# Joining the chunk products of a recurrent scan in pairs of 128 columns, and masking them in another order

## The reference

```python
def rwkv7_step(S, inp):
    r, w, k, v, kk, kka = inp
    sa = jnp.einsum('dbhij,dbhj->dbhi', S, -kk)
    S = S * w[..., None, :] + sa[..., :, None] * kka[..., None, :] + v[..., :, None] * k[..., None, :]
    y = jnp.einsum('dbhij,dbhj->dbhi', S, r)
    return S, y
...
    S0 = jnp.zeros((N_DIR, B, RWKV_HEADS, HEAD_DIM, HEAD_DIM), jnp.float32)
    _, ys = lax.scan(rwkv7_step, S0, xs)
```

## Time and profile before

| | |
|---|---|
| median of 3 runs | 4080.89 us (4072.22 to 4085.7) |
| the profiled execution, first to last instruction | 4081.7 us |
| TensorE busy | 3554.1 us (87%) |
| VectorE busy | 2039.0 us (50%) |
| the scan within it | from about 2995 to 3266 us |

### The profile page before, as it was taken

One profiled execution on the slowest core, in us unless ns is written; L12 is line 12 of the kernel. 1 busy time (PEld: TensorE's weight loads), 2 busy tenths in 40 slices (PEclk: granted clock), 3 DMA queues, 4 the chain that ended last, 5 costly groups with the idle time before them and its releaser, 6 DMA issues. The chain is left out here.

```text
span 4081.7 us, 57350 instructions
## 1 busy us (share of the span) xinstructions
PE 3554.1 (87%) x23427; PEld 2932.0 (72%) x23427; DVE 2039.0 (50%) x2873; ACT 1248.3 (31%) x1650; POOL 0.2 (0%) x4
## 2 busy tenths in 40 slices
PE   7889999997999998799988799968258768979998
PEld 5667888775888776678866688858157746768886
DVE  3475745436665545553443543443655547235334
ACT  2363423324433323332233332222311033214222
POOL 0000000000000000000000000000000000000000
PEclk9999999997999999899989899979579978989998
DMA  3101222220222221122222122212000010112221
GB/s 129 71 0 62 93 94 102 93 93 11 83 100 96 93 84 63 42 73 102 93 83 82 42 93 94 102 58 81 0 8 4 4 42 1 62 62 93 96 100 62
DMA packets 43842, 280.12 MB, mean 69 GB/s; under 512 B 5967, under 2 KB 7119, under 8 KB 11156
## 3 DMA queue, kind: packets, MB, share of 16 engines
q1 hardware_dynamic: 36576, 266.35, 18.4%
q10 hardware_dynamic: 7092, 11.21, 0.8%
HBM read 275.44 MB, written 2.11 MB: 68 GB/s over the span
## 5 line engine op out<-in xcount | busy, mean ns | idle before, releaser
L164 DVE TENSOR_TENSOR WL<-W,WH 128x2048 fp32r<-128x2048 f32 x254 | 582.1, 2292 | 883.2 <-ACT WH L154 877.6
L231 PE MATMUL PS<-XH,WH 128*128 128x512 f32 x2288 | 894.8, 391 | 3.9 <-issue 2.2
L233 PE MATMUL PS<-XH,WL 128*128 128x512 f32 x2288 | 890.3, 389 | 0.0
L232 PE MATMUL PS<-XL,WH 128*128 128x512 f32 x2288 | 890.2, 389 | 0.0
L154 ACT ACTIVATE WH<-W 128x2048 fp32r<-128x2048 f32 x254 | 485.6, 1912 | 1212.1 <-PE PS L321 679.2
L231 PEld LDWEIGHTS PS<-XH,WH 128*128 128x128 f32 x2288 | 429.5, 188 | 99.4 <-issue 10.9
L232 PEld LDWEIGHTS PS<-XL,WH 128*128 128x128 f32 x2288 | 429.5, 188 | 91.1 <-issue 2.2
L233 PEld LDWEIGHTS PS<-XH,WL 128*128 128x128 f32 x2288 | 429.5, 188 | 89.1
L319 PE MATMUL PS<-HH,WH 128*128 128x512 f32 (+1 forms) x1024 | 401.8, 392 | 10.5 <-DVEq L95 9.3
L320 PE MATMUL PS<-HL,WH 128*128 128x512 f32 (+1 forms) x1024 | 400.2, 391 | 0.0
L321 PE MATMUL PS<-HH,WL 128*128 128x512 f32 (+1 forms) x1024 | 400.0, 391 | 0.0
(11 more groups left out here) (444 smaller groups left out, 4395.2 us busy)
## 6 DMA issues: line engine op xcount, KB each, us to landing
W<-in_weights SPq DMA_DIRECT2D x254, 1024.0 KB, 4.8
X<-in_x ACTq DMA_DIRECT2D x1, 2048.0 KB
out<-X ACTq DMA_DIRECT2D x1, 2048.0 KB, 7.1
bias<-bias_spread ACTq DMA_DIRECT2D x4, 256.0 KB
wide_consts<-in_consts ACTq DMA_DIRECT2D x1, 643.0 KB
w_gd<-in_w_gd ACTq DMA_DIRECT2D x1, 640.0 KB
rope<-in_c_rope ACTq DMA_DIRECT2D x1, 528.0 KB
ws<-in_ws ACTq DMA_DIRECT2D x1, 512.0 KB
```

The costliest lines, as they stand in the source:

```text
L164: P.e.tensor_tensor(K.WL[:, s, :], K.W[:, s, :], K.WH[:, s, :].bitcast(F32), ALU.subtract).then_inc(P.sem("weights_split"), P.adds("weight ...
L231: P.e.matmul(out, wh[:, k, c], xh[:, k, r], start=(k == 0), stop=False)
L232: P.e.matmul(out, wh[:, k, c], xl[:, k, r], start=False, stop=False)
L233: last = P.e.matmul(out, wl[:, k, c], xh[:, k, r], start=False, stop=(k == KT - 1))
```

## The change

The products N move to banks 0 and 1, alone. What else is multiplied by b (ab and rb) is now one product of 64 stationary and 2 x 64 streamed columns, issued at the start of the step; and what is multiplied by k (ak and rk) is another, issued after `late_sums`. The 80 operand products of a full step become 48, of which 32 have 128 columns. On VectorE rb is masked right after `state`, without a wait of its own; rk and ak are masked together, after the second `below` is taken. The semaphore `grams_masked` is given after rb, and again after ak.

```diff
+        def grams(left, c):
+
+            for d, F, t, q, cols in each(c):
+                if c < 0:
+                    out, right = K.PS[t, 6 + d, 64 * q:64 * q + 64], src(c, d, "a", F, q)
+                else:
+                    out = K.PS[t, 6 + d, :].rearrange("p (h q n) -> p h q n", h=2, q=4)[:, :, q, :]
+                    right = K.ar[d][F, 0:2, q, self.tokens(c, d)]
+                last = mm(out, src(c, d, left, F, q), right, start=True, stop=True)
+            last.then_inc(P.sem("grams_done"), P.adds("grams_done"))
+
+        def first_grams(c):
+
+            for d, F, t, q, cols in each(c):
+                mm(K.PS[t, d, cols], src(c, d, "a", F, q), src(c, d, "b", F, q), start=True, stop=True)
+            grams("b", c)
...
             if n is not None:
-                fill(("N", "ab"), n, ("rows_ready",) if full else ())
+                if full:
+                    P.e.wait_ge(P.sem("rows_ready"), P.due("rows_ready"))
+                first_grams(n)
...
             if c is not None:
                 late_sums(c)
-            fill(("rb", "ak") if full else ("ak",), n, ("grams_masked",))
+            P.e.wait_ge(P.sem("grams_masked"), P.due("grams_masked"))
+            grams("k", n)
             P.e.wait_ge(P.sem("inverse_ready"), P.due("inverse_ready"))
             below(n)
-            if full:
-                fill(("rk",), n, ("grams_masked",))
             doubled(n)
...
             if c is not None:
                 state(c)
+            if full:
+                masked(K.c_rb, self.two(K, 6, 1, m), K.c_incl[:, 0:m, :], m).then_inc(P.sem("grams_masked"), P.adds("grams_masked"))
+            else:
+                P.e.sem_inc(P.sem("grams_masked"), P.adds("grams_masked"))
+            below(m, 1)
             P.e.wait_ge(P.sem("grams_done"), P.due("grams_done"))
             if full:
-                masked(K.c_rb, self.two(K, 6, 0, m), K.c_incl[:, 0:m, :], m)
-            masked(K.c_ak, self.two(K, 6, 1 if full else 0, m), K.c_strict[:, 1:1 + m, :], m).then_inc(P.sem("grams_masked"), P.adds("grams_masked"))
-            below(m, 1)
-            if full:
-                P.e.wait_ge(P.sem("grams_done"), P.due("grams_done"))
-                masked(K.c_rk, self.two(K, 6, 0, m), K.c_incl[:, 0:m, :], m).then_inc(P.sem("grams_masked"), P.adds("grams_masked"))
+                masked(K.c_rk, self.two(K, 6, 1, m), K.c_incl[:, 0:m, :], m)
+            masked(K.c_ak, self.two(K, 6, 0, m), K.c_strict[:, 1:1 + m, :], m).then_inc(P.sem("grams_masked"), P.adds("grams_masked"))
             doubled(m)
```

More of the change, by code:

```diff
@@ L1801 @@
     HALVES = [slice(0, 64), slice(64, 128)]
-    FILLS = (("N", "ab"), ("rb", "ak"), ("rk",), ("b_rows", "k_rows"), ("v_rows",))
-    META_FILLS = (("N", "ab"), ("ak",), ("b_rows", "k_rows"), ("v_rows",))
     def dirs(self, c):
@@ L1870, in each, with fill_rows @@
             return [(d, F, t, q, slice(64 * q, 64 * q + 64)) for q in range(4) for d, F, t in self.quads(c)]
-        def fill(kinds, c, freed):
-            for name in freed:
-                P.e.wait_ge(P.sem(name), P.due(name))
+        def fill_rows(kinds, c, freed):
+            P.e.wait_ge(P.sem(freed), P.due(freed))
             for half, kind in enumerate(kinds):
@@ L1878, in fill @@
                     out = K.PS[t, 6 + d, 256 * half + 64 * q:256 * half + 64 * q + 64]
[L1879 to L1885, removed]
+                    last = mm(out, src(c, d, kind, F, q), K.ident[F, F], start=True, stop=True)
+            last.then_inc(P.sem("rows_done"), P.adds("rows_done"))
+        def grams(left, c):
[11 more added lines that the diff above has]
+            grams("b", c)
         def right_side(c):
@@ L1966, in pe @@
                 late_sums(c)
-            fill(("rb", "ak") if full else ("ak",), n, ("grams_masked",))
+            P.e.wait_ge(P.sem("grams_masked"), P.due("grams_masked"))
+            grams("k", n)
             P.e.wait_ge(P.sem("inverse_ready"), P.due("inverse_ready"))
             below(n)
-            if full:
-                fill(("rk",), n, ("grams_masked",))
             doubled(n)
-            fill(("b_rows", "k_rows"), n, ("grams_masked",))
+            fill_rows("bk", n, "grams_masked")
             P.e.wait_ge(P.sem("inverse_ready"), P.due("inverse_ready"))
@@ L1976, in pe @@
             doubled(n, not full)
-            fill(("v_rows",), n, ("rows_ready",))
+            fill_rows("v", n, "rows_ready")
             P.e.wait_ge(P.sem("inverse_ready"), P.due("inverse_ready"))
@@ L1996, in begin @@
             P.e.wait_ge(P.sem("grams_done"), P.due("grams_done"))
[L1997 to L2000, removed]
+            masked(K.c_p[:, 1], self.two(K, 0, 0, n), K.c_first[:, 0:n, :], n)
+            masked(K.c_p[:, 0], self.two(K, 6, 0, n), K.c_first[:, 1:1 + n, :], n)
+            masked(K.c_n, self.two(K, 0, 0, n), K.c_strict[:, 0:n, :], n).then_inc(P.sem("dve_order"), P.adds("dve_order"))
+            P.e.wait_ge(P.sem("dve_order"), P.due("dve_order", 0))
             eye = K.c_eye[:, :].rearrange("p (a n) -> p a n", a=1).broadcast_to([128, 4 * n, 64])
```

## The result

The changed kernel took 4097.3 us (median of 5 runs, 4096.32 to 4099.56). The kernel before took 4082.69 us in the same job (5 runs, 4072.22 to 4086.71). The ratio is 1.0039 with a 95% interval of 1.0029 to 1.005: slower by 0.4%, some 15 us, where 20 were forecast. A second job with the same two kernels gave 1.0055 (the third experiment). The profiled execution took 4094.4 us at a mean granted clock of 0.931.

The account below looks back on a forecast made before the run. It took round trips between TensorE and VectorE to bound the scan. Start +3.3, middle +13.4, meta tokens +0.7, issue waits -2.5 and clock +5 gave +20 us on 4080.9, so 4101 us, range 4087 to 4113.

Parts of the forecast that it names:

- Bound: In the scan: neither engine is full; round trips between TensorE and VectorE lie on a step's path of 28.8 us.
- The price of a joined round: TensorE's 32 joined products: streamed columns set the time, 0.90 us a round against 0.98 for two 64-column rounds.
- The first rival: Joined rounds: second 64 columns are free, a round takes 0.49 us; +8 us, 4089, no change; chance 0.13.
- Start of a step: TensorE's products ahead of the first masks take 1.39 us, not 0.98: +0.4 us a step, +3.3 us in all.
- Middle: From c_rb to the second level's sum: `below` waits behind the k round, +1.67 us a step, +13.4 us in all.
- The second rival: Middle of a step: TensorE comes late to the k round anyway, so not slower; -4 us, 4077; chance 0.06.
- Meta chunk: The 16 meta tokens: their ak round now waits for the sum, +0.7 us once.
- Issue waits: TensorE's waits in the scan that the profile names "issue": fewer instructions lessen them, -2.5 us, bounds 0 and -8.3.
- The clock: TensorE's falls to 1.2 GHz in the scan: three more at 1.7 us each, +5 us.
- the third rival: TensorE's clock falls in every step: eight more falls, 13.6 us; +28 us in all, 4109; chance 0.16.

Follow-up runs that it names:

- the third experiment: The changed kernel run again unchanged, beside the kernel before: 4101.78 us, ratio 1.0055.
- Experiment 1: The changed kernel with the second `below` issued ahead of the wait for c_rb and the k round: 4076.52 us, ratio to the kernel before 0.9988.
- experiment 4: The changed kernel with `state` cut in three, its pieces and other work spread over the step's five levels, `below` ahead of each: 4051.27 us, ratio to before 0.9927.
- 5: The kernel of experiment 4 with its joined products split into two of 64 columns: 4065.35 us, ratio to the kernel before 0.9971.
- 8: The kernel of experiment 4 with only the k round split into products of 64 columns: 4058.95 us, ratio to the kernel before 0.9943.
- 9: The kernel of experiment 4 with 16 more unread products of 64 columns in each full step's closing pause: 4062.11 us, ratio to the kernel before 0.9948.
- experiment 6: The kernel of experiment 4 with rb taken out of the step's start and made late in the step: 4056.48 us, ratio to the kernel before 0.9944.
- 2: The changed kernel, order kept, with joined products split again into two of 64 columns: 4105.11 us, ratio to the kernel before 1.0058.
- 10: The kernel of experiment 4 run again unchanged: 4052.74 us, ratio to the kernel before 0.9928.

## Why the prediction held

**Bound.** It held that both engines' round trips, not either engine's busy time, set the scan. Experiment 1 changes no instruction, only a place in the queue, and gets 25 us; experiment 4 gets 50, by order and by cutting `state` in three. In the layout of 4 a second limit shows, the supply of instructions (5, 8 and 9), which the forecast had only as its issue waits.

**The price of a joined round**, forecast 0.90 us from two rows with more columns: 0.87 and 0.92. The first rival (0.49, the second 64 columns free) is refuted.

**Start of a step**, +0.41 us forecast: 1.69 - 1.28 = 0.41 of idle time ahead of the masks. What the forecast missed is the next link: c_pf to the first c_y took 6.97 us on average before and 6.90 after. Before, two falls of the clock and small waits stood there, so the 0.41 shows in full only against the steps without them (experiment 6). The term can't be read apart from those of the issue waits and the clock.

**Middle**, +1.67 us forecast: 4.77 - 3.13 = +1.64, in six of eight steps; the other two (6.19 and 6.27) hold the clock's two falls. Summed over the steps, c_rb to the sum took 28.7 us before and 41.1 after, +12.4 for a forecast of +13.4; the 28.7 contains four steps of 3.62 to 4.82 us, above the 3.13 of an undisturbed one. Experiment 1 shows the cause: with `below` ahead, the term is gone. The second rival, that TensorE comes late to the k round anyway, is refuted by the 2.40 us for which it stands still there. That rival had named its own condition, `below` ahead of the k round, and with it the kernel came to 4076.5 us, where the rival had put 4077. The match is partly luck: the sum then comes 3.13 us after c_rb and not 2.55, since c_rk waits 0.63 for the k round and c_ak stands ahead of the sum too; fewer issue waits (5.2 us in that scan against 11.2) make up for it.

**Meta chunk**, +0.7 forecast: 18.53 - 16.53 = +2.0. The order costs 0.85: from the start of the sum ahead of the k round to the next c_y it takes 2.56 us (3009.43 to 3011.99), where it took 1.71 (3004.41 to 3006.12). The rest is the clock, which the forecast had left out here. The chunk begins at the low level in both kernels, and it comes back to the full one some 13 us behind c_s's memset before the change and some 16 us behind it now.

**Issue waits**, -2.5 forecast, within bounds of 0 and -8.3: 4.6 - 11.2 = -6.6. The forecast had counted 8.3 of the 11.2, on the two lines hit most. Of what the edit itself sets, this is the term that was most mis-sized. Both of its reasons count: in 2, with the new pauses and the old number of records, the waits are 7.4 us; with 512 records fewer they are 4.6 and 3.8.

**The clock**, three more falls and +5 us forecast: the first profile has 2 falls where before had 6, the second has 8. One costs 1.2 us, not 1.7. A stretch in which TensorE is busy for 0.27 of 3.30 us stands right ahead of the fall at 3217. A pause (2.40 us in the step shown, where the forecast had some 3) is now in each step, yet not each is followed by a fall; the third rival's eight more falls are not borne out. The Trainium skill, TensorE: Matmul & The Clock Gate, HAM oscillation, gives the pauses as the reason; the trace agrees as to where the falls are, not as to how often they come. The term's sign stays open: between two executions of one kernel it moved by 7 us, more than the 5 that the forecast had for it.

The sum for the scan: 3.3 + 13.1 + 2.0 - 6.6 = +11.8, and +7.0 with 1.2 for each of the four falls fewer; measured +9.2 in the first profile. In the second, with 3.8 us of issue waits and two falls more, it is 3.3 + 13.1 + 2.0 - 7.4 + 2.4 = +13.4, and measured 277.9 - 261.7 = +16.2. Two to three us of each stay without an account. The medians of the two jobs give +14.6 and +20.3, that is 4097 and 4102, and 4101 lies between them.

The order and the cost in the middle were right, and so was the price of a joined round. That the total of the first job came within 4 us is in part luck: the issue waits came 4 us and the clock 10 us below what was forecast, while 3.5 us of the profiled difference lie outside the scan, and the kernel before came out at 4082.69 in five runs, 1.8 above the base of the forecast.

## What to carry to other kernels

Joining small products saved instructions here, and hardly any array time: it was worth some 14 us, by the medians, where TensorE used its instructions as fast as they came, and some 3 where it waited for another engine. Whoever reorders masks or signals should list what stands behind each wait in the in-order queue; here one item in front of the critical product cost 1.64 us in each of 8 steps, and swapping the two won it back. A step bound by round trips is shortened by laying independent work into each round trip, one piece for each, and not by making pieces shorter.

## What the runs showed of the hardware

TensorE's instructions have a supply limit, and it decides in this scan. The queue named q8 carries instructions in packets of 16 KB (0.70 MB in 43). DMA queues in 3040 to 3220 us, 180 us in the midst of the scan, before:

```profile
q8 instruction: 43, 0.70, 1.7%
```

After the change:

```profile
q8 instruction: 40, 0.66, 1.6%
```

The spread layout with joined products (4):

```profile
q8 instruction: 48, 0.79, 1.8%
```

The spread layout with split products (5) has the same row, word for word. The windows of that stretch, TensorE's records first, kernel 4:

```profile
3040.00:3220.00 180.00, 162.88 (x6105) 155.95 (x6096) 110.04 (x175) 21.05 (x41) 0.00 (x0) 1.00 0.02 5
```

Kernel 5:

```profile
3040.00:3220.00 180.00, 158.13 (x6272) 150.41 (x6268) 104.14 (x165) 20.67 (x40) 0.00 (x0) 1.00 0.02 5
```

A packet goes with 12,201 / 48 = 254 records of TensorE (matmuls and weight loads) in kernel 4 and with 261 in kernel 5. All six kernels of the spread layout (4, 5, 6, 8, 9 and 10), whatever instructions they hold, get 47 or 48 packets in these 180 us, 3.75 us a packet, and 6102 to 6272 matmul records; before and after, which pause more, take 43 and 40. Nowhere in the twelve traces, which hold 133 to 137 of these packets each, do two begin less than 3.2 us apart. From 3040 to 3220 us they follow each other after 3.2 to 4.6 us in the spread layout, and after up to 6.4 before and 8.5 after the change. A stretch in which four quarters work at 64 columns uses up a packet's 128 matmul records in about 2 us (64 of them took 0.98), so it outruns the supply by a factor of nearly two, and pauses must make up for it. That the limit is the supply, and not the array, is shown by experiments 5, 8 and 9; that it is the transfer of these packets, and not something behind it, is inferred from the equal counts and the least distance alone, and is not shown. It also gives the joined product nearly all of its worth: in it, half as many instructions keep the array busy for the same time.

An estimate puts the size beside it: at the 6105 records in 180 us of kernel 4, the 256 matmul records more of 8 and 9 need 7.5 us. Their scans are 7.5 and 8.7 us longer (234.8 and 236.0 against 227.3). For the 512 more of 5 the estimate is 15 us; the medians show 14, the profiled scans 7 to 10.
